# The V and B projections as a fourth Strassen-Winograd pair in a float32 hybrid-layer kernel

## The chip, the cores and the metric

The kernel runs on one core of a Trainium2 chip. A core has five engines with a queue each: TensorE (PE), VectorE (DVE), ScalarE (ACT), GpSimd (POOL) and SyncE (SP, which here only issues transfers). Each works off its own queue strictly in order and waits on semaphores. The time is the device time of one execution in microseconds.

## What is computed

One layer of a hybrid decoder for a prompt of 1024 tokens and eight samples of one new token each, all in float32. D_MODEL is 1024, there are 8 heads of 64.

```python
def _mixer_layer(x, c, conv_prev, attend, w_ada, b_ada, g_pre, w_in, conv_w, g_conv, b_sb, g_attn, w_out, g_post):
    shift, scale, gate = jnp.split(jax.nn.silu(c) @ w_ada + b_ada, 3, axis=-1)
    h = _rmsnorm(x, g_pre) * (1 + scale[:, None]) + shift[:, None]
    p = h @ w_in                                       # 1024 x 4096
    hc, bc, cc, gc, q, k, v, ga = jnp.split(p, _split_points(), axis=-1)
    u = cc * hc
    u_pad = jnp.concatenate([conv_prev.astype(u.dtype), u], axis=1)
    conv_y = sum(conv_w[i] * u_pad[:, i:i + L] for i in range(CONV_WIDTH))
    ya = _rmsnorm(bc * conv_y, g_conv) * jax.nn.silu(gc)
    o = attend(q, k, v, b_sb).reshape(Bsz, L, ATT_DIM)
    yb = _rmsnorm(o, g_attn) * jax.nn.silu(ga)
    m = jnp.concatenate([ya, yb], axis=-1) @ w_out
    y = x + gate[:, None] * _rmsnorm(m, g_post)
```

`attend` is stick-breaking attention: scores z, then exp(log_sigmoid(z) + the sum of log_sigmoid(-z) over the later keys), then times v. For the samples K and V are 4096 past rows, gathered page by page from a cache of 134 MB in use. Besides y, the kernel returns k, v and the last rows of u.

## The kernel before

**Layout.** `hT` holds h with channels on partitions: 8 blocks (K tiles) of 128 channels by 1032 columns (1024 tokens and 8 samples). Work goes through four groups g of 128 output channels (two heads). Each group needs eight projections of h, each with a 1024 x 128 slab of w_in, held in four slots of `wsl`: Q, K, V, GC, GA, HC, CC, BC (here: B).

**Seven-product pairs.** In before, six of the eight are made in three pairs: Q with K, GC with GA, HC with CC. A pair is a 2 x 2 block product by the Strassen-Winograd scheme: instead of eight block products it makes seven. The sums of h (T1 to T4, in `xT4`) are made once by DVE; the sums of the weights (S1, S2, S4 and a difference in place, 128 x 512 each) are made for each pair by POOL in `weight_sum`, four operations. The 1032 columns of a half are cut in two, so a pair has two chunks. `product(i, j)` is product j of chunk i: four matmul calls of 258 columns, into the PSUM bank `BANK[j]`. They come in the order 1, 5, 2, 6, 3, 7, 4. ACT takes products 1, 5, 2, 6 and 4 out of PSUM (`evac_st`), DVE takes 3 and 7 and adds (`product_sum`). Product 4 of a chunk waits for DVE's sum of its 7 (semaphore `d_c22`), product 5 of the next for the sum of its 3 (`d_c12`), product 2 for ACT's copy of 1 (`st_seed`).

**V and B.** V is made in before with tokens on partitions (`values`: 64 calls of 128 columns and 8 for the sample rows), since attention wants it so. B is a plain projection (`project_b`: 3 column chunks x 8 K tiles, 344 columns each).

**The program of a group.** PE's `body` has a head (t = 0 to 7) and then slots 8 to 33, where u = t - 8 numbers 24 units of attention. In the head of group 1 to 3 PE makes the Q/K pair (`EARLY`) and V; in a slot it makes scores, P.V (`outputs`), the transposes of weights (`turn`), pieces of products (`pieces_at`); in slots 32 and 33 and behind them stands B. In the first group the head projects Q and K plainly. Samples run beside it: SP loads K and V pages into `ring`, POOL multiplies a K pair by the query (`prod`, 128 x 1024), DVE reduces it (`reduce_pair`), two pairs a slot in slots 0 to 5 and then about one; PE multiplies V pages (`value_quad`). DVE also does each unit's clamp, scan and subtraction, and, in t = 0 to 6 of a head, the six `gating` steps for the group before. `gates` makes the adaLN gate, in the first group at t = 0 and 5.

Nothing is scheduled by a program: the order on each engine is the order of these loops. Behind group 3 stands the output projection: `out_unit` n makes half a token tile from 8 blocks of `yT` with 8 blocks of w_out (`wo`). The blocks of groups 0 to 2 were written to `y_parts` in memory and are loaded again.

The code below has the functions that the diff touches.

## Time and profile before

| | us |
|---|---|
| median of 3 runs | 828.92 |
| lowest, highest | 827.64, 829.51 |
| the profiled execution | 829.45 |
| its span in the trace | 827.7 |
| PE busy | 786.0 |
| DVE busy | 537.8 |
| POOL busy | 429.5 |
| ACT busy | 352.2 |

The page of the profile gives busy times by engine, the timeline gives each instruction's start and length, with the idle time before it and what ended that in brackets. A line number names the line that issues it; L1359 is the helper that issues every matmul of PE, so operations are told apart by their operands. One matmul call of float32 shows as two instructions in the trace (16 calls as x32). On PE a row's length runs a little over into the next row's start, so durations here are taken from start to start. The granted clock is 1.00 in all stretches between 60 and 787 us.

### The profile page before, as it was taken

The page shows a single profiled execution, that of the slowest core. Times are in us where ns is not written, and L with a number is a line of the kernel's source. Part 1 is how long each engine was busy: PE and PEld are TensorE (multiplying, and loading weights), DVE is VectorE, ACT ScalarE, POOL GpSimd, SP SyncE. Part 2 cuts the span into 40 slices and gives each one's busy share as a digit, 9 for nine tenths or more (in the row PEclk, how much of TensorE's full clock was granted, in tenths as well). Part 3 has the DMA queues.
Part 4 walks back from the last instruction along what each step waited for, and adds up shares of the span by engine and source line. Part 5 has one row for each costly group of instructions (what it writes and reads, how often), then busy time and mean ns, then how long its engine had stood idle before and what let it go on. Part 6 is the DMA issues. An engine that isn't in the chain of part 4 may idle for free.

```text
span 827.7 us, 14401 instructions
## 1 busy us (share of the span) xinstructions
PE 786.0 (95%) x4397; PEld 522.3 (63%) x4397; DVE 537.8 (65%) x728; ACT 352.2 (43%) x729; POOL 429.5 (52%) x230
## 2 busy tenths in 40 slices
PE   0889989999999999999999999999999999999995
PEld 0455766766787666768866766788676665444442
DVE  3575679787585888848748877585788854232344
ACT  7311065775122667821155676112567731122122
POOL 0105896474787566666966485588665630100000
PEclk9989999999999999999999999999999999999998
DMA  8998777577789888786998776868978797554001
GB/s 317 359 340 293 224 229 223 177 239 230 239 256 305 268 257 266 242 253 211 299 282 262 244 259 222 274 212 289 302 250 255 232 332 304 166 182 163 27 27 53
DMA packets 131071, 197.85 MB, mean 239 GB/s; under 512 B 10025, under 2 KB 51030, under 8 KB 130994
## 3 DMA queue, kind: packets, MB, share of 16 engines
q1 hardware_dynamic: 99512, 181.11, 66.5%
q10 hardware_dynamic: 31482, 15.82, 6.8%
q8 instruction: 35, 0.57, 0.3%
q14 instruction: 42, 0.34, 0.1%
HBM read 185.25 MB, written 11.66 MB: 238 GB/s over the span
## 4 chain that ended last, share of the span: by engine, by line
PE 79%; issue 5%; DMA 5%; DVE 4%; POOL 3%; SPq 2%; ACT 0%; ACTq 0%; POOLq 0%; DVEq 0%
PE ps L1359 76%; DMA ring<-in_w_ada_dram 4%; PE ps L1599 3%; POOL prod L617 2%; SPq L386 1%; DVE ps L1243 1%; DMA ring<-in_cache_k_dram 1%; SPq L378 1%; DVE zd L1219 1%; DVE zc L1249 0%; POOL wsl L600 0%; DVE rows L1062 0%; DMA ring<-in_cache_v_dram 0%; DVE zc L1229 0%; POOL spd L560 0%
## 5 line engine op out<-in xcount | busy, mean ns | idle before, releaser
L617 POOL TENSOR_TENSOR prod<-ring,qb 128x1024 f32<-128x1024 f32 x128 | 308.7, 2430 | 195.2 <-DMA ring<-in_cache_k_dram 92.0
L1359 PE MATMUL ps<-hT,wsl 128*128 128x258 f32 (+1 forms) x640 | 174.7, 419 | 0.1
L1219 DVE TENSOR_REDUCE zd<-prod 128x16 f32<-128x1024 f32 x128 | 154.3, 1213 | 26.0 <-POOL prod L617 25.4
L1359 PEld LDWEIGHTS ps<-hT,wsl 128*128 128x128 f32 x640 | 119.1, 190 | 53.3 <-issue 18.6
L1359 PE MATMUL ps<-ring,apad 128*32 128x512 f32 x592 | 84.4, 650 | 9.0 <-DMA ring<-in_w_ada_dram 7.5
L1359 PE MATMUL ps<-xT,wS 128*128 128x258 f32 x352 | 92.2, 385 | 0.0
L1359 PE MATMUL ps<-xT,wsl 128*128 128x258 f32 x352 | 89.5, 386 | 0.0
L1229 DVE TENSOR_SCALAR zc<-ps,bsb 128x512 f32<-128x512 f32 (+3 forms) x96 | 54.8, 612 | 42.0 <-PE ps L1359 41.7
L657 ACT ACTIVATE rise<-ps,bsh 128x512 f32<-128x512 f32 (+3 forms) x96 | 55.5, 578 | 45.9 <-DVE zc L1229 45.8
L1359 PEld LDWEIGHTS ps<-xT,wsl 128*128 128x128 f32 x352 | 62.9, 190 | 18.7 <-issue 8.0
L657 ACT ACTIVATE av<-ps 128x512 f32<-128x512 f32 (+3 forms) x96 | 46.8, 488 | 63.4 <-PE ps L1599 62.9
L1243 DVE TENSOR_TENSOR_SCAN ps<-rise,ps 128x512 f32<-128x512 f32 (+3 forms) x64 | 65.5, 1023 | 11.8 <-ACT ps L657 11.8
L1359 PEld LDWEIGHTS ps<-xT,wS 128*128 128x128 f32 x352 | 62.2, 190 | 15.4 <-issue 8.7
L1359 PEld LDWEIGHTS ps<-wsl,hT 128*128 128x128 f32 (+1 forms) x576 | 63.3, 181 | 7.6 <-issue 6.4
L1359 PE MATMUL ps<-wsl,hT 128*128 128x128 f32 (+1 forms) x576 | 66.7, 276 | 0.6 <-ACT bcb L657 0.6
L1249 DVE TENSOR_TENSOR zc<-zc,ps 128x512 f32<-128x512 f32 (+3 forms) x96 | 52.9, 551 | 2.2
L1599 PE MATMUL ps<-ident,zc 128*128 128x128 f32 x288 | 47.7, 275 | 6.6 <-DVE zc L1249 6.6
L650 POOL TENSOR_TENSOR rs<-ss,half 128x1 f32<-128x1 f32 x8 | 4.3, 544 | 90.0 <-DVE ss L1341 90.0
L657 ACT ACTIVATE sp<-zc 128x512 f32<-128x512 f32 (+3 forms) x96 | 49.7, 518 | 0.0
L657 ACT ACTIVATE ps<-sp 128x512 f32<-128x512 f32 (+3 forms) x96 | 47.5, 495 | 3.0
L1599 PEld LDWEIGHTS ps<-ident,zc 128*128 128x128 f32 x288 | 36.0, 141 | 19.4 <-DVE zc L1249 11.3
L1359 PEld LDWEIGHTS ps<-av,vN 128*64 128x64 f32 x576 | 30.5, 136 | 27.6 <-issue 25.8
(241 smaller groups left out, 1012.7 us busy)
## 6 DMA issues: line engine op xcount, KB each, us to landing
ring<-in_cache_k_dram SPq DMA_DIRECT2D x256, 256.0 KB, 3.5
ring<-in_cache_v_dram SPq DMA_DIRECT2D x256, 256.0 KB, 3.2
wsl<-in_w_in_dram ACTq DMA_DIRECT2D x30, 512.0 KB, 6.5
ring<-in_w_ada_dram SPq DMA_DIRECT2D x5, 2048.0 KB, 14.7
xT<-in_x_prompt_dram SPq DMA_DIRECT2D x2, 2048.0 KB, 10.9
out_dram<-oT SPq DMA_DIRECT2D x8, 512.0 KB, 5.0
ring<-in_x_prompt_dram SPq DMA_DIRECT2D x8, 512.0 KB, 7.2
xT<-y_parts SPq DMA_DIRECT2D x6, 512.0 KB, 9.5
```

What stands on the lines that cost most here:

```text
L378: _, numbers = nc.values_load_multi_w_load_instructions(pages[0:1, bass.ds(seq * PAGES + (PAGES - 2 - r), 2)], engines=[mybir.EngineType.S ...
L386: sp_e.dma_start(dst[:, j, :], src).then_inc(full, 16)
L617: pool.tensor_tensor(prod[:, p % 2].rearrange("p (j c) -> p j c", j=2), kring[:, p % 4], qb[:, p // 16].unsqueeze(1).to_broadcast([P, 2, H ...
L650: pool.tensor_tensor(rs[:, 20 + t % 2:21 + t % 2], ss[:, 20 + t % 2:21 + t % 2], half[:, 0:1], ALU.pow).then_inc(m_rstd, 1)
L657: nc.scalar.activation(out, in_, func, **kw).then_inc(done, 1)
L1219: v.tensor_reduce(zd[:, t // 16, :, r:r + 2], prod[:, t % 2].rearrange("p (j h d) -> p h j d", j=2, h=NH), AX_X, ALU.add)\
L1229: v.tensor_scalar(zc[:, u % 3, lo:QC], ps[:, Z + u % 3, 0:QC - lo], bsb[:, bass.ds(2 * g + h, 1)], CLAMP, ALU.add, ALU.min).then_inc(zc_re ...
L1243: v.tensor_tensor_scan(back(sums), back(rise[:, par_, lo + 1:QC + 1]), back(sums), start, ALU.add, ALU.add).then_inc(scan_done, 1)
L1249: v.tensor_tensor(zc[:, u % 3, lo:QC], zc[:, u % 3, lo:QC], sums, ALU.subtract)\
L1359: return nc.tensor.matmul(out, l, r, start=start, stop=stop, skip_group_check=True)
L1599: last = nc.tensor.transpose(ps[:, Z + u % 3, P * j:P * (j + 1)], zc[:, u % 3, lo + P * j:lo + P * (j + 1)], ident[:, :])
```

## The change

V and B become a fourth pair. A group now has four pairs and eight chunks: Q/K, V/B, GC/GA, HC/CC. `values`, `project_b` and their copies `evac_v` and `evac_b` go. V now comes out with channels on partitions (`vT`, over `av`), and is transposed by PE in eight 128 x 128 blocks and one of 8 rows (`value_rows` at t = 7 and 9, into bank Z+2, copied by ACT in `value_rows_copy`). The weight sums of V/B are made by DVE (`value_weight_sum`), the other three pairs' by POOL.

Products 1, 5, 2, 6 of the next group's first chunk (`AHEAD`) take B's place in slots 32, 33 and behind; the other 24 and product 1 of chunk 4 stand in the head. In the last group the first two blocks of `out_unit(2)` stand at slot 32. In the first group the second `gate_sums` stands behind product 1 of chunk 2. Two parts of `y_parts` and two slabs of w_out are loaded in slots 30 and 26 of the last group, the others in another order; three parts go to `kring` and not to `yT`. The attention weights of the samples are packed so that the matmuls of V pages have 8, 16, 24 or 32 columns of weights instead of 32, which leaves one clearing copy per eight samples' sequences out.

```diff
-EARLY = ((), (1, 5), (2, 6), (3, 7, 11), (4, 15), (12, 16), (13, 17))
+AHEAD = (1, 5, 2, 6)
+EARLY = ((3, 7, 11), (4, 15, 12, 16), (13, 17, 21), (14, 25, 22, 26), (23, 27, 31), (24, 35), (32, 36), (33, 37))
+EARLY_FIRST = {6: (21, 25, 22, 26, 23, 27, 31), 7: (24, 35, 32, 36, 33, 37)}
+TAKEN = {1: (4, 11, 15, 12, 16), 3: (14, 21, 25, 22, 26), 5: (24, 31, 35), 6: (32, 36)}
+TAKEN_FIRST = {6: (21, 25, 22, 26), 7: (24, 31, 35, 32, 36)}
+SUMMED = {1: 0, 3: 1, 5: 2, 8: 3}
+SUMMED_FIRST = {7: 2, 8: 3}
...
+            def value_weight_sum(g, step):
+                n = PAIRS * g
...
+                if step == 0:
+                    v.wait_ge(w_full[3], 16 * (2 * g + 1))
+                    v.wait_ge(q_out, 16)
+                    if n:
+                        v.wait_ge(st_full[5], 2 * n)
+                    v.tensor_tensor(S1, a21, a22, ALU.add).then_inc(vb_sum, 1)
+                if step == 1:
+                    v.wait_ge(w_full[2], 16 * (2 * g + 1))
+                    v.wait_ge(vb_sum, 4 * g + 1)
+                    if n:
+                        v.wait_ge(st_full[6], 2 * n)
+                    v.tensor_tensor(S2, S1, a11, ALU.subtract).then_inc(vb_sum, 1)
+                if step == 2:
+                    if n:
+                        v.wait_ge(st_full[3], 2 * n)
+                    v.wait_ge(vb_sum, 4 * g + 2)
+                    v.tensor_tensor(S4, a12, S2, ALU.subtract).then_inc(vb_sum, 1)
+                if step == 3:
+                    v.tensor_tensor(a21, a11, a21, ALU.subtract).then_inc(vb_sum, 1)
...
-                    if not first and t in (4, 6):
-                        product_sum(g, first, t // 6, 3)
-                        product_sum(g, first, t // 6, 7)
+                    chunk = (SUMMED_FIRST if first else SUMMED).get(t)
                     if u > 0 and u % 6 == 0:
...
+                        chunk = 3 + u // 6
+                    if chunk is not None:
+                        product_sum(g, first, chunk, 3)
+                        product_sum(g, first, chunk, 7)
+                    if t in (2, 3):
+                        value_weight_sum(g, 2 * (t - 2))
+                        value_weight_sum(g, 2 * (t - 2) + 1)
...
+                if not last:
+                    weight_sum(g + 1, 0, 0)
+                    weight_sum(g + 1, 0, 1)
                 silu_mul(g, 1)
                 decode_scores(g, 1, first)
                 if not last:
-                    weight_sum(g + 1, 0, 0)
+                    weight_sum(g + 1, 0, 2)
                 decode_softplus(g, 1)
                 if not last:
-                    weight_sum(g + 1, 0, 1)
+                    weight_sum(g + 1, 0, 3)
...
+                    elif last_:
+                        if u == NU:
+                            out_unit(2, (0, 1), True)
                     else:
-                        project_b(u - NU, range(0, 4))
+                        product(g + 1, 0, AHEAD[2 * (u - NU)])
...
+                    if last and t == SLOTS - 2:
+                        sp_e.wait_ge(part_out, 32 * (GROUPS - 1))
+                        sp_e.wait_ge(st_full[5], ALL)
+                        load_part(0, 0)
+                        load_part(0, 1)
+                    if last and t == 26:
+                        sp_e.wait_ge(st_full[2], CHUNKS * GROUPS - 4)
+                        load_wo(WO_ORDER[0])
+                        sp_e.wait_ge(st_full[4], CHUNKS * GROUPS - 4)
+                        load_wo(WO_ORDER[1])
...
+            sp_e.wait_ge(part_out, 32 * (GROUPS - 1))
+            sp_e.wait_ge(prod_ready, 32 * GROUPS - 3)
+            load_part(1, 0)
+            sp_e.wait_ge(prod_ready, 32 * GROUPS - 2)
+            load_part(1, 1)
             sp_e.wait_ge(z_full, NU * GROUPS)
-            load_wo(WO_ORDER[0])
-            load_wo(WO_ORDER[1])
...
             load_wo(WO_ORDER[2])
             load_wo(WO_ORDER[3])
```

**Place 1: DVE in the head of group 1**, t = 1 to 3 of its loop. `zd<-prod` is a reduction for a K pair, `qT` and `kT<-ps,stage` are the sums of products 3 and 7 of a chunk, `last` to `hcb<-hcb,bcb` step 2. Before:

```order
L1219 TENSOR_REDUCE zd<-prod 128x8x2 [waits prod_ready] x2
L1180 SCALAR_TENSOR_TENSOR last<-naught,ub 128x2
L1183 COPY tail<-last 128x2 [waits last_ready]
L1184 COPY samp<-ub 128x8
L1185 COPY samp<-gcb 128x8
L1186 COPY samp<-gab 128x8
L1188 COPY samp<-bcb 128x8 [waits pj_free]
L1189 TENSOR_TENSOR hcb<-hcb,bcb 128x1024
L1219 TENSOR_REDUCE zd<-prod 128x8x2 [waits prod_ready,bconv_ready]
L1219 TENSOR_REDUCE zd<-prod 128x8x2 [waits prod_ready]
L1095 SCALAR_TENSOR_TENSOR qT<-ps,stage 128x258 [waits e_u2,st_full3]
L1102 TENSOR_TENSOR kT<-ps,stage 128x258 [waits e_p5,st_full7]
```

And after, where `wS` and `wsl` are the weight sums of V/B:

```order
L1135 TENSOR_TENSOR wS<-wsl 128x512 [waits st_full5,q_out,w_full3]
L1141 TENSOR_TENSOR wS<-wS,wsl 128x512 [waits st_full6,vb_sum,w_full2]
L1291 TENSOR_REDUCE zd<-prod 128x8x2 [waits prod_ready] x2
L1251 SCALAR_TENSOR_TENSOR last<-naught,ub 128x2
L1254 COPY tail<-last 128x2 [waits last_ready]
L1255 COPY samp<-ub 128x8
L1256 COPY samp<-gcb 128x8
L1257 COPY samp<-gab 128x8
L1259 COPY samp<-bcb 128x8 [waits e_c21]
L1260 TENSOR_TENSOR hcb<-hcb,bcb 128x1024
L1163 SCALAR_TENSOR_TENSOR qT<-ps,stage 128x250 [waits e_u2,st_full3,bconv_ready]
L1170 TENSOR_TENSOR kT<-ps,stage 128x258 [waits e_p5,st_full7]
```

The sum of chunk 1's product 7 (the last row) stands behind two weight sums that wait for PE (`st_full5`, `st_full6`) and behind gating step 2. On PE, at the same place, from product 6 of chunk 1 through products 3 and 7 and product 1 of chunk 2 to product 4 of chunk 1, which waits for that sum (`d_c22`):

```order
L1431 MATMUL ps<-xT,wS 128x258 x4
L1431 MATMUL ps<-hT,wS 128x258 [waits e_p5]
L1431 MATMUL ps<-hT,wS 128x258 x3
L1431 MATMUL ps<-xT,wsl 128x258 [waits e_u2]
L1431 MATMUL ps<-xT,wsl 128x258 x3
L1431 MATMUL ps<-hT,wsl 128x258 [waits e_c11,w_full2]
L1431 MATMUL ps<-hT,wsl 128x258 x3
L1431 MATMUL ps<-xT,wsl 128x258 [waits d_c22]
L1431 MATMUL ps<-xT,wsl 128x258 x3
```

**Place 2: DVE in the first group's head**, t = 0 to 7. `rows`, `ub` and `gab` are the gate's steps. Before, 10 reductions and then the gate:

```order
L1219 TENSOR_REDUCE zd<-prod 128x8x2 [waits prod_ready] x10
L1060 TENSOR_TENSOR rows<-ps,ub 8x512 [waits gate_ps]
L1062 TENSOR_TENSOR rows<-rows,wS 8x512 [waits gate_step]
L1065 TENSOR_TENSOR ub<-ps,ub 128x512 [waits gate_ps,gate_step]
L1067 TENSOR_TENSOR wS<-wS,ub 128x512 [waits gate_step]
L1069 MEMSET ssa 128x1024
L1219 TENSOR_REDUCE zd<-prod 128x8x2 [waits prod_ready,ssa_zero]
L1219 TENSOR_REDUCE zd<-prod 128x8x2 [waits prod_ready] x2
```

After, with four weight sums between the reductions, and the sums of chunk 2 (`av`, `bcb`) behind the gate:

```order
L1146 TENSOR_TENSOR wS<-wsl,wS 128x512 [waits vb_sum]
L1148 TENSOR_TENSOR wsl<-wsl 128x512
L1291 TENSOR_REDUCE zd<-prod 128x8x2 [waits prod_ready] x6
L1101 TENSOR_TENSOR rows<-ps,ub 8x512 [waits gate_ps]
L1103 TENSOR_TENSOR rows<-rows,gab 8x512 [waits gate_step]
L1106 TENSOR_TENSOR ub<-ps,ub 128x512 [waits gate_ps,gate_step]
L1108 TENSOR_TENSOR gab<-gab,ub 128x512 [waits gate_step]
L1110 MEMSET ssa 128x1024
L1291 TENSOR_REDUCE zd<-prod 128x8x2 [waits prod_ready,gate_step]
L1291 TENSOR_REDUCE zd<-prod 128x8x2 [waits prod_ready]
L1166 TENSOR_TENSOR av<-ps,stage 128x258 [waits e_u2,st_full3]
L1170 TENSOR_TENSOR bcb<-ps,stage 128x258 [waits e_p5,st_full7]
```

What moved: V had no sum on DVE; now product 4 of chunk 2 on PE waits for the last row.

**Place 3: PE at slots 32 and 33 of the last group.** `hT,wsl 128x344` is B, `ring,apad` V pages, `av,vN` P.V, `spd` the samples' cumulation. Before:

```order
L1359 MATMUL ps<-av,vN 64x128 x8
L1359 MATMUL ps<-ring,apad 32x512 x4
L1359 MATMUL ps<-hT,wsl 128x344 x4
L1599 MATMUL ps<-ident,zc 128x128 x4
L1359 MATMUL ps<-xT,wsl 128x258 x4
L1359 MATMUL ps<-hT,wsl 128x344 x4
L1359 MATMUL ps<-ring,apad 32x512 x4
L1359 MATMUL ps<-hT,wsl 128x344 x8
L1359 MATMUL ps<-av,vN 64x128 x8
L1359 MATMUL ps<-hT,wsl 128x344 x8
L1359 MATMUL ps<-spd,ntri 128x256
L1359 MATMUL ps<-spd,nones 128x256
```

After, `wsl,xT` to `kT,ring` are two blocks of `out_unit(2)`, whose operands SP loads:

```order
L1431 MATMUL ps<-ring,apad 16x512 x4
L1431 MATMUL ps<-wsl,xT 128x512
L1431 MATMUL ps<-wsl,ring 128x512
L1431 MATMUL ps<-qT,xT 128x512
L1431 MATMUL ps<-kT,ring 128x512
L1592 MATMUL ps<-ident,zc 128x128 x4
L1431 MATMUL ps<-xT,wsl 128x258 x4
L1431 MATMUL ps<-ring,apad 16x512 x4
L1431 MATMUL ps<-av,vN 64x128 x8
L1431 MATMUL ps<-spd,ntri 128x256
L1431 MATMUL ps<-spd,nones 128x256
L1431 MATMUL ps<-wsl,xT 128x512
```

B is gone from here, and two blocks of the output projection stand ahead of the turn, of product 4 and of the cumulation.

## Rows read from the trace of the kernel before

**Rows 1.** The page, part 1: busy us, share of the span, instructions per engine.
```profile
PE 786.0 (95%) x4397; PEld 522.3 (63%) x4397; DVE 537.8 (65%) x728; ACT 352.2 (43%) x729; POOL 429.5 (52%) x230
```

**Rows 2.** Who waited for whom, PE: us in total, times, longest us.
```profile
PE ps L1599 <- DVE zc L1249: 6.6, 8, 1.5
```

**Rows 3.** Timeline, PE, end of group 0 and group 1: start us, us, operation, count.
```profile
210.37 1.09 PE L1359 MATMUL ps<-av,vN 128*64 128x128 f32 x16
...
217.35 7.38 PE L1359 MATMUL ps<-wsl,hT 128*128 128x128 f32 x64 [0.20 <-ACT bcb L657]
224.66 1.13 PE L1359 MATMUL ps<-ring,apad 128*32 128x512 f32 x8
225.72 2.01 PE L1359 MATMUL ps<-hT,wsl 128*128 128x258 f32 x8
227.56 1.90 PE L1359 MATMUL ps<-xT,wS 128*128 128x258 f32 x8
229.30 1.90 PE L1359 MATMUL ps<-hT,wsl 128*128 128x258 f32 x8
...
259.93 1.91 PE L1359 MATMUL ps<-wsl,hT 128*8 128x128 f32 x16
261.77 0.66 PE L1631 MATMUL ps<-ident,kT 128*128 128x128 f32 x4
```

**Rows 4.** Timeline, DVE, head of group 1.
```profile
221.75 2.54 DVE L1177 SCALAR_TENSOR_TENSOR gab<-oT,par,gab 128x1024 f32<-128x1024 f32 x1
...
227.68 1.16 DVE L1180 TENSOR_TENSOR_SCAN last<-naught,ub 128x2 f32<-128x2 f32 x1
228.88 2.28 DVE L1183 COPY tail<-last 128x2 f32<-128x2 f32 x1
...
232.61 2.35 DVE L1219 TENSOR_REDUCE zd<-prod 128x16 f32<-128x1024 f32 x2
234.87 0.42 DVE L1095 SCALAR_TENSOR_TENSOR qT<-ps,stage 128x258 f32<-128x258 f32 x1
```

**Rows 5.** Timeline, DVE and POOL, head of group 0.
```profile
96.52 0.68 DVE L1060 TENSOR_TENSOR rows<-ps,ub 8x512 f32<-8x512 f32 x1 [0.47 <-PE ps L1359]
...
102.52 2.34 DVE L1219 TENSOR_REDUCE zd<-prod 128x16 f32<-128x1024 f32 x2
...
76.25 23.17 POOL L617 TENSOR_TENSOR prod<-ring,qb 128x1024 f32<-128x1024 f32 x10 [3.27 <-DVE zd L1219]
```

**Rows 6.** Timeline, PE, first group: V, gate sums, slots 9 and 11.
```profile
87.67 7.41 PE L1359 MATMUL ps<-wsl,hT 128*128 128x128 f32 x64
...
95.45 2.08 PE L1359 MATMUL ps<-ssa,e 128*8 128x512 f32 x4
...
111.74 0.33 PE L1599 MATMUL ps<-ident,zc 128*128 128x128 f32 x1 [0.85 <-DVE zc L1249]
...
117.98 0.44 PE L1599 MATMUL ps<-ident,zc 128*128 128x128 f32 x2 [1.27 <-DVE zc L1249]
```

**Rows 7.** Timeline, ACT, group 2, slots 7 and 9.
```profile
415.49 0.60 ACT L657 ACTIVATE vN<-ps 128x512 f32<-128x512 f32 x1 [10.54 <-PE ps L1359]
...
424.92 0.26 ACT L657 ACTIVATE av<-ps 128x128 f32<-128x128 f32 x1
```

**Rows 8.** SP, PE and POOL timelines and DMA issues (median us to landing), last group.
```profile
665.66 0.43 SPq L392 DMA_DIRECT2D qT<-in_w_out_dram  x1
...
668.76 2.58 PE L1359 MATMUL ps<-hT,wsl 128*128 128x344 f32 x8
...
677.76 1.46 POOL L560 TENSOR_TENSOR spd<-spd,om 128x256 f32<-128x256 f32 x1 [7.26 <-ACT om L657]
...
xT<-y_parts SPq DMA_DIRECT2D x6, 512.0 KB, 9.5
...
wsl<-in_w_out_dram SPq DMA_DIRECT2D x3, 512.0 KB, 7.8
...
qT<-in_w_out_dram SPq DMA_DIRECT2D x1, 512.0 KB, 4.6
```

493 lines of the change are left out of this document (239 added, 254 removed).

## The prediction

> **What bounds the kernel now.** First the busy times: PE works 786.0 us, 95% of the span, DVE 537.8 and POOL 429.5 [rows 1]. Then PE's waits: the largest entry that another engine causes is 6.6 us in eight waits, all for the subtraction that DVE makes for a unit's turn [rows 2]. The reader is to see that PE hardly waits: a matmul taken out shortens the kernel by nearly its time, and a wait put in front of PE lengthens it by its time. So the question is first how much PE work goes, and then which new waits of PE the new order on DVE, ACT and SP makes. For the second, the timelines of the engines around the edited places are laid over the new orders.
>
> The sum is made against the profiled execution, 829.45 us. The median of the three runs is 828.92, so the last step takes off 0.53.
>
> **PE's work.** A row runs by 0.17 or so into the next (2.01 at 225.72 against 1.84 to the next start [rows 3]). B is 24 calls, 48 instructions; 8 of them are 2.58 [rows 8] less 0.17, so B is 6 x 2.41 = 14.5 us a group. V is 64 instructions twice and 16 once: 217.35 to 224.66 is 7.31, 259.93 to 261.77 is 1.84 [rows 3], in all 16.5. Together 31.0 go. Two chunks of seven products come: a product takes from 227.56 to 229.30, 1.74 [rows 3], 14 are 24.4. Nine transposes of V come; four are 0.66 long [rows 3] less 0.17, so 0.12 each and 1.1 in all. A group saves 31.0 - 24.4 - 1.1 = 5.5, the four groups **22.0 us**. This term has one answer. The narrower weights of the page matmuls change nothing that I count: their cost lies in the 512 columns streamed, 1.06 for eight from 224.66 to 225.72 [rows 3].
>
> **DVE in the heads of groups 1 to 3** (place 1). DVE now makes V/B's second weight sum only when PE has finished product 6 of chunk 1, and sum 7 of chunk 1 stands behind it, behind two reductions and behind gating step 2. PE has three products left by then, 3 and 7 of chunk 1 and 1 of chunk 2, 3 x 1.74 = 5.2 us, and then product 4 waits for that sum. DVE needs: the weight sum, 512 columns; a sum of 258 columns takes 0.42 [rows 4], so I estimate 0.65; two reductions 2.35 [rows 4]; gating step 2 from 227.68 to 232.61, 4.93 [rows 4]; two sums at 0.42, 0.84. That is 8.8. PE waits 8.8 - 5.2 = 3.6 us, in three groups **10.7 us**. Queued behind the waiting DVE instruction is all of this, and PE alone waits for it. Before, the same sum had slack, since V's 7.31 us stood in PE's queue there. The unsure piece is the 4.93: a scan of two elements takes 1.16 in it and a copy of two elements 2.28 [rows 4]. Such small ones are long while POOL multiplies, and end as its instruction ends. Were POOL idle, neither need be longer than the 0.42 of a 258-column sum; step 2 is then 4.93 - 3.44 + 0.84 = 2.3, DVE needs 6.2 and PE waits 1.0. Bounds for the three groups: 3.0 to 10.7. I take the upper end, because POOL multiplies K pairs throughout that head as before and the rows are from the same place.
>
> **The first group's head** (place 2). There V stood in PE's queue from 87.67 [rows 6]. Now, from there: product 1 of chunk 2 (1.74), one more call of 258 columns (a quarter product, 0.44), the gate sums (2.08 at 95.45, less the 0.17: 1.9 [rows 6]), products 5, 2, 6, 3, 7 (8.7), product 1 of chunk 3 (1.74): 102.2. Then product 4 of chunk 2 waits for DVE's two sums. These stand behind gate step 2, which took from 96.52 to 102.52, and two reductions, 2.34 [rows 5]: 104.9, with the sums 105.7. PE waits 3.5. But DVE also has four weight sums of 512 columns between its reductions now. POOL's ten products there run without a gap, 23.17 us, 2.32 each [rows 5], and a reduction leaves DVE about 1.1 us between two. A step with two SBUF operands, started beside such a product, was long: gating step 1 took 2.54 in group 1 [rows 4]. If the four weight sums take turns with POOL's products, each puts the chain of products and reductions back by about half a product, 4 x 1.16 = 4.6, of which the 0.47 that DVE idled before the gate [rows 5] is to spare: 4.1, and PE waits 3.5 + 4.1 = 7.6. In return PE's waits of 0.85 and 1.27 in slots 9 and 11 [rows 6], 2.1 together, go: they are DVE's backlog behind the gate, which by then is worked off while PE waits. Net **5.5 us**, bounds 1.4 (no turns) and 5.5. I take 5.5, since the 2.54, the 1.16 and the 2.28 all show turns.
>
> The Trainium skill, "SBUF — State Buffer", section on the two separate sides, says that VectorE and GpSimd share a port pair under an exclusive lock held for a whole instruction, and that a VectorE operation with two SBUF inputs needs it while a reduction does not. The 2.54, 1.16 and 2.28 [rows 4] agree, and so do reductions that stay at 1.17 each. By that rule the wait in the first group is 7.6; without it it is 3.5, and the sum of all terms 4.1 us lower.
>
> **Slot 10.** ACT now copies V's four transposed tiles in one operation there; the like copy took 0.60 at 415.49 [rows 7]. It stands behind the copy of the weights, 0.26 at 424.92 [rows 7], and PE's next scores wait for the bank that it empties. PE's queue has nothing to put between, so I charge the copy whole: 4 x 0.60 = **2.4 us**. The lower bound is 0, if ACT has taken it before the weights come.
>
> **The end of the last group** (place 3). B was what PE did while SP's loads for the output projection landed. Now two blocks of it stand at 668.76 [rows 8], where B's first eight instructions were. Two parts and two w_out slabs come early; the other two parts and slabs 1 and 5 are issued where the first slab was, from 665.66. The first of such a row landed after 4.6, later ones after 7.8 [rows 8]. The fourth, issued 0.9 later, is there at 674.4. PE has done 1.7 us of blocks at 670.5 and waits 3.9. Then come the blocks left, 1.7, the turn, 0.5, product 4, 1.74, a page group, 1.06, and P.V, about 1.0 [rows 3, 8]: 680.4, and PE's cumulation needs POOL's 1.46 us product of 677.76, which followed ACT's logarithms [rows 8]. ACT takes product 4 out before them; that copy can now start only at 678.3, and with 0.4 for it, 1.6 for the four functions and 1.46 for POOL the operand is there at 681.8. PE waits 1.4 more. **5.3 us**, bounds 0.7 (the fourth lands after 4.6, no second wait) and 7.0 (it lands after 9.5, as loads of parts did [rows 8]). I take the row of the nearest position in the queue.
>
> Costed at nothing: POOL loses four of its weight sums a group; SP's earlier loads in slots 26 and 30 cover the same bytes; the clearing copies that go were not on PE's path. If DVE's longer queue in the heads reached slot 8, that would cost; see the slow rival.
>
> **The sum.** 829.45 - 22.0 + 10.7 + 5.5 + 2.4 + 5.3 = 831.35, and 0.53 off is **830.8 us**.
>
> **Rivals.** (1) *The waits are light.* DVE's steps run at their undisturbed times, where the columns allow, the loads land early, and slot 10 costs nothing: 828.9 - 22.0 + 3.0 + 1.4 + 0 + 0.7 is 812.0; with DVE's term in the heads at full size, or with the three others so, it is 819 to 821, with one more 824. For it speaks that POOL has less to do in the head than before, against it the three long rows. (2) *No new waits at all*, the pure saving: 828.9 - 22.0 = 806.9; for it only that PE's waits were tiny so far. (3) *Between*, 824 to 827: the DVE term is at two thirds. (4) *Slower: DVE does not recover by slot 8.* In a head of groups 1 to 3 DVE gets two weight sums in a row in t = 2 and two in t = 3, beside 16 reductions of 1.17 and the gating. If each waits out a whole product of POOL, 2.32, instead of half, PE's wait at chunk 1 grows by 2.3 us, and the first clamp of slot 8 comes, by my estimate, 1 us late: 3.3 in three groups is 9.9, so 840.7. It decides from the point where a weight sum takes over 1.2 us on average. For it: the copy of two elements that took 2.28 [rows 4]. Against it: POOL too waits for DVE's reductions and then leaves gaps. (5) The change not doing what it says is excluded as far as products go: the calls are in the order.
>
> **How the numbers follow.** A measurement of this kernel tells 0.2%, 1.7 us, from no change, so no change is 827.3 to 830.6. The forecast's own range is 827.3 to 835, chance 0.40, of it 0.18 within no change and 0.22 above. Rival 1 has 0.20 and rival 3 0.14, both faster; rival 2 and the lowest part of rival 1 have 0.07, faster. Rival 4, 836 to 841, has 0.15. The 0.04 left go to no change. Faster 0.41, no change 0.22, slower 0.37. The range from 819.0 to 838.0 holds all but rival 2, the lowest part of rival 1 and the upper half of rival 4.
>
> **What would show it.** PE's busy time down by about 22, products at 1.74. In groups 1 to 3 a row of PE with about 3.6 us idle before product 4 of chunk 1, ended by DVE's sum. In the first group 3.5 (no turns) or 7.6 (turns) before product 4 of chunk 2, with DVE's weight sums 0.65 or well over 1 us. No wait of 0.85 and 1.27 in slots 9 and 11. In slot 10 about 0.6, ended by ACT's copy of V. In the last group about 3.9 us before the third or fourth block, ended by a load, and about 1.4 before the cumulation. The forecast is wrong first if gating step 2 is much shorter than 4.93 in the new order, since most of what eats the saving hangs on it and on the 7.6.

## The result and the profile after

| | before | after |
|---|---|---|
| median, us | 829.21 | 845.62 |
| lowest, highest (4 runs each) | 827.64, 830.87 | 845.47, 846.80 |
| span of the profiled execution | 827.7 | 843.9 |
| PE busy | 786.0 | 776.7 |
| span less PE busy | 41.7 | 67.2 |
| mean granted clock of TensorE | 0.992 | 0.976 |

The ratio is 1.0193, with a 95% interval of 1.0174 to 1.0212: the change makes the kernel slower by 1.9%. The page of the kernel after, part 1, busy us per engine, answers to [rows 1]:

```profile
PE 776.7 (92%) x4113; PEld 515.0 (61%) x4113; DVE 563.6 (67%) x760; ACT 359.2 (43%) x749; POOL 433.2 (51%) x230
```

PE is busy 9.3 us less and idle 25.5 us more. That makes the 16.2 us of the span. The view of PE's waits (us in total, times, longest), which answers to [rows 2], names the idle time:

```profile
PE ps L1431 <- DVE kT L1170: 11.4, 3, 3.8
...
PE ps L1592 <- DVE zc L1321: 10.1, 8, 2.5
PE ps L1431 <- DVE bcb L1170: 7.7, 1, 7.7
...
PE ps L1431 <- DMA ring<-y_parts: 3.3, 1, 3.3
...
PE ps L1431 <- issue: 1.1, 1, 1.1
```

The three waits of 3.8 us for the sum of product 7 of chunk 1 (kT), the one of 7.7 us in the first group (bcb), and the 3.3 and 1.1 us at the end of the last group were not there before. The waits for the turn's operand went from 6.6 to 10.1 in all.

PE's busy time holds the surprise. 22.0 us less work were forecast, 9.3 less are seen. The timeline of PE in the first group and in group 2 (start us, us, operation, count, in brackets the idle time before it) shows where the rest is:

```profile
109.26 3.81 PE L1431 MATMUL ps<-xT,wsl 128*128 128x258 f32 x8 [7.71 <-DVE bcb L1170]
112.86 2.28 PE L1431 MATMUL ps<-xT,wS 128*128 128x258 f32 x8
114.98 1.90 PE L1431 MATMUL ps<-hT,wsl 128*128 128x258 f32 x8
```

```profile
408.42 3.81 PE L1431 MATMUL ps<-xT,wsl 128*128 128x258 f32 x8 [3.81 <-DVE kT L1170]
412.02 2.88 PE L1431 MATMUL ps<-xT,wS 128*128 128x258 f32 x8
414.74 1.90 PE L1431 MATMUL ps<-hT,wsl 128*128 128x258 f32 x8
```

A product at full speed takes 1.74 from start to start, as in [rows 3]. Behind the wait of 7.71 the first one takes 3.60 (109.26 to 112.86) and the second 2.12. Behind the 3.81 of group 2 they take 3.60 and 2.72. The windows of group 2 (us; busy us of PE, PEld, DVE, ACT, POOL; then the granted clock, the DMA share and GB/s) show the clock:

```profile
402.00:404.00 2.00, 2.00 (x10) 1.74 (x10) 1.97 (x3) 0.00 (x0) 2.00 (x2) 1.00 0.90 313
404.00:406.00 2.00, 0.61 (x3) 0.19 (x1) 2.00 (x1) 0.00 (x0) 2.00 (x1) 1.00 0.57 152
406.00:408.00 2.00, 0.00 (x0) 0.00 (x0) 1.97 (x8) 0.00 (x0) 0.14 (x1) 0.79 0.51 187
408.00:410.00 2.00, 1.58 (x4) 1.30 (x5) 2.00 (x5) 0.00 (x0) 0.00 (x0) 0.50 0.81 242
...
412.00:414.00 2.00, 2.00 (x6) 1.61 (x5) 0.78 (x1) 0.76 (x2) 2.00 (x2) 0.50 0.71 253
414.00:416.00 2.00, 2.00 (x10) 1.75 (x10) 0.91 (x2) 0.39 (x1) 2.00 (x2) 1.00 0.86 242
```

PE stops at 404.6. The clock is 1.00 up to 406, falls while PE waits (0.79 in 406 to 408) and is 0.50, the lower of the two levels (1.2 GHz), until 414, 5.6 us into the work. Then it is 1.00 again. Over all places where it is low behind a wait, start to start against 1.74 a product (0.86 a block of the output projection): 2.2 us in the first group, 1.5, 2.8 and 2.9 in groups 1 to 3, 1.8 in the last group's end. Another 1.7 is lost at 724 to 728, just behind the samples' sums of one column, behind no wait. Together 12.9, and 22.0 - 12.9 is the 9.1 that PE's busy time fell.

That last 1.7 costs the kernel little. Behind the same place the kernel before waits for a V page, and the kernel after, which comes there later, does not (first before, then after):

```profile
714.41 1.13 PE L1359 MATMUL ps<-ring,apad 128*32 128x512 f32 x8 [1.53 <-DMA ring<-in_cache_v_dram]
```

```profile
731.02 1.06 PE L1431 MATMUL ps<-ring,apad 128*8 128x512 f32 x8
```

The Trainium skill, "TensorE: Matmul & The Clock Gate", part 1, says that the array runs at half clock by default and that activity releases it, so that idle gaps bring the lower clock back and work behind them starts slow. The rows agree: 0.50 behind the wait of 3.81 in group 2.

DVE's timeline in the head of group 1 is what [rows 4] were before:

```profile
241.80 0.69 DVE L1141 TENSOR_TENSOR wS<-wS,wsl 128x512 f32<-128x512 f32 x1 [2.12 <-PE ps L1431]
...
244.66 1.47 DVE L1251 TENSOR_TENSOR_SCAN last<-naught,ub 128x2 f32<-128x2 f32 x1
246.17 2.27 DVE L1254 COPY tail<-last 128x2 f32<-128x2 f32 x1
...
250.23 0.42 DVE L1170 TENSOR_TENSOR kT<-ps,stage 128x258 f32<-128x258 f32 x1
...
280.63 0.61 DVE L1301 TENSOR_SCALAR zc<-ps,bsb 128x128 f32<-128x128 f32 x2 [2.63 <-PE ps L1431]
```

Gating step 2 (from the scan at 244.66 to the sums) lies between the reductions and the sum of product 7 at 250.23, just as it was forecast: 5.2 us long (249.90, where the sums begin, less 244.66) where 4.93 was charged, with the same two-element copy of 2.27. The last row is the first clamp of slot 8, which waits 2.63 us for PE: DVE was not late there.

In the first group's head ([rows 5]) the four weight sums of V/B, 128 x 512 each, lie between the reductions:

```profile
77.24 1.99 DVE L1135 TENSOR_TENSOR wS<-wsl 128x512 f32<-128x512 f32 x1
79.33 2.66 DVE L1141 TENSOR_TENSOR wS<-wS,wsl 128x512 f32<-128x512 f32 x1
...
84.17 2.00 DVE L1146 TENSOR_TENSOR wS<-wsl,wS 128x512 f32<-128x512 f32 x1
86.09 2.84 DVE L1148 TENSOR_TENSOR wsl<-wsl 128x512 f32<-128x512 f32 x1
```

They take 1.99 to 2.84, and the second one of group 1, at 241.80 with POOL idle, takes 0.69. They did take turns with POOL's products, as the prediction chose. At the end of the last group, where [rows 8] had B:

```profile
696.52 1.29 PE L1431 MATMUL ps<-wsl,xT 128*128 128x512 f32 x2 [3.33 <-DMA ring<-y_parts]
...
707.23 0.67 PE L1431 MATMUL ps<-spd,ntri 128*128 128x256 f32 x2 [1.13 <-issue]
```

The wait of 3.33 is ended by the load of a part, and it stands ahead of the first block and not ahead of the third or fourth, where it was forecast. The code says why: a part's load for either half of the channels counts up the same semaphore (`part_in[k]`), and block 0 waits until both have come, so the load issued in slot 30 alone does not let it start. The other was issued at 690.16, and the block starts 6.4 us later. The fourth block has its operands in time.

### The profile page after: what moved, and what is told of

The parts are those of the page before. It is cut to its first block, busy times and chain, and to the rows that moved or that the text cites. A ratio compares the mean times of both kernels' runs of the same rounds, so it can differ in the third digit from the quotient of the medians.

```text
span 843.9 us, 13952 instructions
## 1 busy us (share of the span) xinstructions
PE 776.7 (92%) x4113; PEld 515.0 (61%) x4113; DVE 563.6 (67%) x760; ACT 359.2 (43%) x749; POOL 433.2 (51%) x230
## 4 chain that ended last, share of the span: by engine, by line
PE 70%; DVE 10%; issue 7%; DMA 4%; SPq 4%; POOL 3%; ACT 1%; POOLq 0%; DVEq 0%; ACTq 0%
PE ps L1431 66%; PE ps L1592 3%; DVE zd L1291 2%; POOL prod L659 2%; DMA xT<-in_x_prompt_dram 2%; SPq L413 1%; SPq L405 1%; DMA ring<-in_w_in_dram 1%; DVE ps L1315 1%; DMA ring<-y_parts 1%; DMA ring<-in_cache_k_dram 1%; DVE xT L1066 1%; POOL wsl L644 1%; DVE wS L1141 1%; DVE last L1251 0%
## 5 line engine op out<-in xcount | busy, mean ns | idle before, releaser
L1431 PE MATMUL ps<-hT,wsl 128*128 128x258 f32 (+1 forms) x576 | 145.7, 397 | 0.3 <-DVE zb L1189 0.3
L1431 PE MATMUL ps<-xT,wsl 128*128 128x258 f32 x480 | 127.7, 403 | 19.2 <-DVE kT L1170 11.4
L1431 PEld LDWEIGHTS ps<-hT,wsl 128*128 128x128 f32 x576 | 107.8, 191 | 33.1 <-issue 12.0
L1431 PE MATMUL ps<-xT,wS 128*128 128x258 f32 x480 | 125.2, 391 | 0.0
L1431 PEld LDWEIGHTS ps<-xT,wsl 128*128 128x128 f32 x480 | 91.2, 199 | 47.2 <-DVE kT L1170 12.7
L1431 PEld LDWEIGHTS ps<-xT,wS 128*128 128x128 f32 x480 | 88.5, 195 | 20.9 <-issue 10.1
L1431 PE MATMUL ps<-ring,apad 128*32 128x512 f32 (+3 forms) x592 | 81.8, 632 | 7.2 <-DMA ring<-in_w_ada_dram 7.1
L702 ACT ACTIVATE av<-ps 128x512 f32<-128x512 f32 (+4 forms) x104 | 49.9, 480 | 84.0 <-PE ps L1592 70.6
L1431 PE MATMUL ps<-hT,wS 128*128 128x258 f32 x240 | 62.3, 391 | 0.0
L1592 PE MATMUL ps<-ident,zc 128*128 128x128 f32 x288 | 47.8, 275 | 10.1 <-DVE zc L1321 10.1
L1431 PEld LDWEIGHTS ps<-hT,wS 128*128 128x128 f32 x240 | 42.5, 190 | 19.0 <-issue 14.6
## 6 DMA issues: line engine op xcount, KB each, us to landing
ring<-in_w_ada_dram SPq DMA_DIRECT2D x5, 2048.0 KB, 14.3
xT<-in_x_prompt_dram SPq DMA_DIRECT2D x2, 2048.0 KB, 11.2
```

The source lines that it names most:

```text
L702: nc.scalar.activation(out, in_, func, **kw).then_inc(done, 1)
L1431: return nc.tensor.matmul(out, l, r, start=start, stop=stop, skip_group_check=True)
L1592: last = nc.tensor.transpose(ps[:, Z + u % 3, P * j:P * (j + 1)], zc[:, u % 3, lo + P * j:lo + P * (j + 1)], ident[:, :])
```

## The experiments

Each kernel was timed beside the kernel before on the same chip. The differences below are between medians. They come from three chips, on which the kernel before took 829.57 (the runs up to all three places mended), 830.74 (the transfers moved, and the narrow weights) and 829.00 (the rest). Where versions from different chips are compared, the difference of their ratios, taken on 829 us, is given too. Fills and moves are told from the changed kernel (845.6).

### The waits filled with work

```diff
-                        product(g, code // 10, code % 10)
+                        product(g, code // 10, code % 10, again={21: 0 if first else 2, 31: 4 if first else 0}.get(code, 0))
...
-                for k in ks:
+                for k in list(ks) * (1 + again):
```

> The changed kernel, but PE makes product 1 of V/B's second chunk three times over in groups 1 to 3, and product 1 of the third chunk five times over in the first group: 2 x 1.74 us in place of each wait of 3.8 us, 4 x 1.74 in place of the 7.7. The repeats overwrite the same bank, so nothing else changes. Theory A (a wait of PE is paid a second time, because TensorE's granted clock is at half speed for some us behind it): the waits become work of the same length and the slow matmuls behind four of the five waits, 2.2 + 1.5 + 2.8 + 2.9 = 9.4 us by the profile of the changed kernel, go. About 836. Theory B (PE's surplus of 12.7 us has another cause, and a matmul more is only a matmul more): 845 to 846, since work stands where a wait stood.

Measured 839.96, ratio to before 1.0128 [1.0104, 1.0151], 5.7 less than the changed kernel though PE has ten products, 17.4 us, more to make. Its timeline of PE in group 1 (the repeats, then product 4):

```profile
246.95 5.38 PE L1431 MATMUL ps<-hT,wsl 128*128 128x258 f32 x24
252.68 2.01 PE L1431 MATMUL ps<-xT,wsl 128*128 128x258 f32 x8 [0.35 <-DVE kT L1170]
```

Product 4 at 252.68 now takes 1.85 from start to start behind a wait of 0.35. Work in place of a wait made the kernel faster, which theory B excludes. The gain is less than the 9.4 of theory A: PE's busy time rose by 13.1 (to 789.8), not by 17.4 - 9.4 = 8.0. Of the missing 5.1, 1.7 is slow clock behind a wait of 2.45 us in slot 13 of the first group, after which the clock did not fall in the changed kernel (2.54 there), and some 3.3 is slow clock in the prologue of this execution, ahead of the edit (32 small matmuls there took 5.88 in place of 3.92, 16 of another kind 3.30 in place of 1.92).

### DVE's sums ahead of gating step 2

```diff
-SUMMED = {1: 0, 3: 1, 5: 2, 8: 3}
+SUMMED = {1: 0, 5: 2, 8: 3}
...
+                    if not first and t == 2:
+                        product_sum(g, first, 1, 3)
+                        product_sum(g, first, 1, 7)
                     if not first and t in GATING_AT:
```

> The changed kernel with one edit: in groups 1 to 3 DVE makes the two sums of V/B's... rather of chunk 1 (Q/K) ahead of gating step 2, not behind it. DVE is through with its reductions at 244.66 in the profile of the changed kernel, PE has product 7 done at 245.0 and wants the sum at 246.7. Theory A: the three waits of 3.8 us (11.4) go, and with them the slow clock behind them (7.2): 845.6 - 18.6 = 827. Theory B: only the waits go: 834. Theory C (DVE is the bound in the head and the wait comes back at the next sum or in slot 13): 840 or more.

Measured 841.84, ratio 1.0151 [1.0129, 1.0173]: only 3.8 less. The waits of PE:

```profile
PE ps L1595 <- DVE zc L1324: 13.9, 8, 4.1
PE ps L1434 <- DVE bcb L1170: 10.7, 4, 7.7
```

The entry for kT is gone, as it should. But the waits for the turn's operand rose from 10.1 to 13.9, most of it in slot 13 (4.1, 3.1 and 2.7 in groups 1 to 3, against 1.6, 1.9 and 1.9), and a wait of 1.0 in each of these groups came for the sum of chunk 2, behind gating step 3 (bcb, 10.7 in all with the 7.7). The clock now falls to 0.50 behind slot 13. So the gain was given back some 46 us later (the wait of 3.8 began at 246.9 in group 1, the one of 4.1 at 293.3), wait and slow clock together: theory C, in another place than the next sum.

### DVE's sums ahead of the second gate step, first group

```diff
-SUMMED_FIRST = {7: 2, 8: 3}
+SUMMED_FIRST = {8: 3}
...
+                    if first and t == 5:
+                        product_sum(g, first, 2, 3)
+                        product_sum(g, first, 2, 7)
                     if first and t in (0, 5):
                         gates(t // 5)
```

> The changed kernel with one edit: in the first group DVE makes the two sums of chunk 2 ahead of the second gate step, not behind it. Theory A: the wait of 7.7 us shrinks to 0.5 (DVE can start the second sum at about 101.4) and the 2.2 us of slow clock go: 845.6 - 9.4 = 836. Theory B: only the wait goes: 838.4. The gate step then comes 1.5 us later; if PE's transposes of K wait for it, or DVE's backlog grows by slot 13, some of it comes back (up to 2).

Measured 837.06, ratio 1.0090 [1.0065, 1.0115]: 8.6 less, between A's 9.4 and B's 7.2. In the profile the wait of 7.7 has no row left, and the clock is 1.00 between 60 and 240 us. Nothing came back in this group.

### All three places mended

```diff
-                    elif last_:
-                        if u == NU:
-                            out_unit(2, (0, 1), True)
-                    else:
+                    elif not last_:
                         product(g + 1, 0, AHEAD[2 * (u - NU)])
...
-                if not last_:
+                if last_:
+                    out_unit(2, (0, 1), True)
+                else:
                     product(g + 1, 0, AHEAD[3])
                 cumulate(1)
```

with the two edits above.

> Both edits of DVE's order, and the two blocks of the output projection moved from slot 32 of the last group to just ahead of the last cumulation, where their loads have landed. Theory A: all of 11.4 + 7.2, 7.2 + 2.2 and about 4.4 + 1.8 go: 845.6 - 34 = 811 to 813. Theory B: only waits go: 845.6 - 23 = 822.6. Theory C (new waits behind the removed ones): above 825.

Measured 828.05, ratio 0.9977 [0.9949, 1.0004], not to be told from before, and its ten runs spread from 821.4 to 830.7, for a reason that the one trace kept does not show. Against theory A 15 us are missing. PE waits 14.6 us for the turn's operand, up to 3.8 in slot 13 of each group. The chain there, in group 1, read backwards. PE, DVE and POOL in their timelines:

```profile
289.54 0.55 PE L1598 MATMUL ps<-ident,zc 128*128 128x128 f32 x3 [3.77 <-DVE zc L1327]
```

```profile
286.81 1.22 DVE L1297 TENSOR_REDUCE zd<-prod 128x16 f32<-128x1024 f32 x1 [4.29 <-POOL prod L659]
```

```profile
277.82 1.27 POOL L644 TENSOR_TENSOR wsl<-wsl 128x512 f32<-128x512 f32 x1
284.44 2.34 POOL L659 TENSOR_TENSOR prod<-ring,qb 128x1024 f32<-128x1024 f32 x1 [5.35 <-issue]
```

PE waits for DVE's subtraction, DVE's reduction at 286.81 waited 4.29 for POOL's product, and POOL stood from 279.1 to 284.4 with nothing that the profile names. Its operand is a pair of K pages. SP's queue and ACT's, and the issues of 272 to 276 with their KB and median us to landing:

```profile
274.58 0.43 SPq L479 DMA_DIRECT2D out_dram<-vN  x1
276.24 4.51 SPq L413 DMA_DIRECT2D ring<-in_cache_k_dram  x4
```

```profile
273.40 0.38 ACTq L767 DMA_DIRECT2D wsl<-in_w_in_dram  x1
```

```profile
wsl<-in_w_in_dram ACTq DMA_DIRECT2D x1, 512.0 KB, 8.2
out_dram<-vN SPq DMA_DIRECT2D x1, 512.0 KB, 8.4
```

The pages are issued from 276.24. Just ahead of them go the store of V's rows (the vN row) and a load of weights, 512 KB each, which take over 8 us here (6.1 and 4.7 in the kernel before). In the kernel before, the store stood at 267.57 and the load at 261.88, and pages issued at 269.21 let POOL start at 273.70, 4.5 us after their issue against 8.2 here. The store stood as close ahead of the pages then (1.6 us) as it does now (1.7). What moved is the load: 7.3 us ahead of the pages before, 2.8 now, since its slab is free only when chunk 3 is done. So two transfers and not one stand right ahead of the pages of slots 11 and 12.

### The two transfers moved, each alone and together

```diff
-                    if t == 10:
+                    if t == 14:
                         sp_e.wait_ge(pj_free, PJ * g + 2)
```

> The version with all three edits (a_all3), and SP's store of V's rows (512 KB) moved from slot 10 to slot 14, behind the K page loads of slots 11 to 13. In a_all3 PE waits 14.6 us in eight waits for the turns, 2.1, 3.8, 3.5 and 3.2 us of it in slot 13 of each group; there DVE's reduction waits 4.3 us for POOL's product, and that for a K page pair, which lands 8.2 us after its issue, behind the store of V at 274.6 and a load of weights at 273.4. Theory D1 (the store is what delays the pages): the slot 13 waits fall to 1 us or less and the slow clock behind them goes: 828 - 9 - 7 = 812. Theory D2 (the load of weights does): same as a_all3. Theory E (DVE or POOL have too much work in slots 8 to 13): same as a_all3.

```diff
-                    if i == 3:
+                    if i == 4:
                         load_w(g, CC_, 3)
```

> The version with all three edits (a_all3), and ACT's load of the CC weights (512 KB) issued before its copy of product 4 of chunk 4 (about slot 14) and not of chunk 3 (slot 10). Theory D2 (that load delays the K pages of slots 11 and 12): slot 13 waits fall, 812 to 818. Theory D1 (the store does) and theory E (DVE's or POOL's work): same as a_all3.

```diff
-SUMMED = {1: 0, 5: 2, 8: 3}
+SUMMED = {1: 0, 8: 3}
...
-                    if not first and t == 2:
-                        product_sum(g, first, 1, 3)
-                        product_sum(g, first, 1, 7)
+                    if not first and t in (2, 4):
+                        product_sum(g, first, t // 2, 3)
+                        product_sum(g, first, t // 2, 7)
```

> Both of these moves, and DVE's sums of chunk 2 ahead of gating step 3 (PE waits 1.0 us there in each of groups 1 to 3 in a_all3). Theory D1 or D2: at least the better of the two, less 3 us: 808 to 812. Theory E: 825.

| | median | ratio to before | waits for the turn's operand |
|---|---|---|---|
| all three mended | 828.05 | 0.9977 [0.9949, 1.0004] | 14.6 |
| and the store later | 818.99 | 0.9870 [0.9823, 0.9918] | 8.2 |
| and the load later | 814.01 | 0.9783 [0.9748, 0.9818] | 8.4 |
| and both, and the sums of chunk 2 | 812.85 | 0.9782 [0.9744, 0.9820] | 5.7 |

The waits are those of the profiled execution. For the version with the load moved that was the slowest of five (819.32), with 3.3 of its 8.4 in one wait in group 2. By the ratios, on 829 us, moving the store gains 8.9 and moving the load 16.1. Moving either transfer brings most of the waits down, and neither D1 nor D2 holds alone, since each expected nothing of the other move: the pages were late because two transfers of 512 KB stood ahead of them. With both moved, and the sums of chunk 2, the time is not to be told from the load moved alone (0.9782 and 0.9783). Theory E falls, since no engine has less work in these three kernels. POOL in the best one, at the same place (the weight sum, then the product that was at 284.44, 4.6 us behind its pages' issue at 274.40), and its waits of PE:

```profile
276.78 1.27 POOL L644 TENSOR_TENSOR wsl<-wsl 128x512 f32<-128x512 f32 x1
279.04 2.38 POOL L659 TENSOR_TENSOR prod<-ring,qb 128x1024 f32<-128x1024 f32 x1 [0.99 <-issue]
```

```profile
PE ps L1598 <- DVE zc L1327: 5.7, 8, 1.1
...
PE ps L1437 <- DMA rise<-in_w_out_dram: 1.3, 1, 1.3
```

This version beats both kernels: 17.9 us or 2.2% less than the kernel before on the same chip. From PE's first scores of one group to those of the next it takes 152.3 and 153.3 us (265.48, 417.76, 571.03) where the kernel before took 157.2 and 157.9, so a group gained 4.8 of the 5.5 us that its products save.

### A wait put back, short and long

```diff
+                    for i in range(more):
+                        v.tensor_tensor(S2, S1, a11, ALU.subtract).then_inc(vb_sum, 1)
+                        v.wait_ge(vb_sum, at + 2 + i)
                     v.tensor_tensor(S2, S1, a11, ALU.subtract).then_inc(vb_sum, 1)
```

with more = 3 and 8 in groups 1 to 3, in the best version; the counts that DVE and PE wait for are raised to match. The run with 8 is told first. Its expectation says "the same" of the edit with 3, whose expectation stands behind it.

> The same with nine in place of one: the sum comes 5.6 us later, PE waits some 4.4 us three times. Theory A: 13.2 of waits and 2.9 of slow clock behind each (as behind the waits of 3.8 in the changed kernel): 812.9 + 13.2 + 8.6 = 834.7. Theory B (a wait is paid once): 826. If DVE's delay reaches slots 8 to 13, both more.

Measured 829.07, ratio 1.0015 [0.9997, 1.0034]: 16.2 more than the best version. PE waits 4.39 three times, 13.2:

```profile
239.84 3.60 PE L1442 MATMUL ps<-xT,wsl 128*128 128x258 f32 x8 [4.39 <-DVE kT L1175]
243.24 2.04 PE L1442 MATMUL ps<-xT,wS 128*128 128x258 f32 x8
245.11 1.90 PE L1442 MATMUL ps<-hT,wsl 128*128 128x258 f32 x8
```

The two products behind the wait take 3.40 and 1.87, 1.8 us more than two at full speed. So each of these waits cost 4.4 and about 1.8 more where I expected 2.9, and 13.2 + 5.4 is 18.6 against 16.2 between the medians (16.0 between the spans; two rows of the prologue took 3.5 longer in the best version's profiled execution, 3.64 against 1.92 and 5.52 against 3.71). The clock falls behind every one of them. The two versions ran on different chips. By their ratios (1.0015 and 0.9782, with intervals of 0.0018 and 0.0038 to either side) the difference is 19.3 us, give or take 3.5 by my estimate from these intervals. That holds the 18.6 and leaves out theory B's 13.2. Theory A holds in kind, with a second price that varies from 1.5 to 2.9 us in these traces.

> The best version so far (b_best, 812.9 us), in which PE waits nowhere over 1.4 us between 60 and 800 us, and DVE makes V/B's second weight sum four times over in groups 1 to 3 (the same result, each about 0.7 with its semaphore). The sum of product 7 of chunk 1 then comes 2.1 us later, some 1.0 after PE wants it. Theory A' (a short wait is paid once, only a long one is paid twice): 812.9 + 3.0 = 816. Theory A'' (any wait lowers the clock): 816 + 3 x 2 = 822.

Measured 820.29, ratio 0.9890 [0.9865, 0.9914]: 7.4 more than the best version, 9.0 by the ratios, where A' expected 3.0 and A'' 9.

```profile
PE ps L1603 <- DVE zc L1332: 9.6, 13, 1.9
...
PE ps L1442 <- DVE kT L1175: 2.3, 3, 0.8
```

The waits put in are 0.75 each, 2.3 in all, and the clock is 1.00 behind them: A'' falls, though its sum came nearer to the time. For PE also waits 3.9 us more for the turn's operand, in 13 places and not 8, with one of 1.9 at 296.4, behind which the clock falls (1.7 us). PE's first scores of group 1 come 0.9 us later than in the best version (266.39 against 265.48), and the K pages of 283.76 are asked for 1.7 us later, at 285.42. That is seen. Why it costs more than the shift of 4.4 us in the run above (5.6 for the turn's operand) stays open.

### The output blocks back at slot 32

The best version without the move of out_unit(2).

> b_best with the two blocks of the output projection back at slot 32 of the last group, as in the changed kernel. Theory A: a wait of 3.3 to 4.5 us for the parts and 1.1 for the cumulation come back, with 1.8 us of slow clock: 812.9 + 6.5 = 819. Theory B (only the wait): 817.5. If the loads are in time here, 813.

Measured 817.07, ratio 0.9845 [0.9813, 0.9876], 4.2 more than the best version, 5.2 by the ratios. The waits of PE:

```profile
PE ps L1437 <- DMA ring<-y_parts: 4.5, 1, 4.5
...
PE ps L1437 <- issue: 1.1, 1, 1.1
```

The wait for the part and the one for the cumulation are back, 5.6 together, and the clock is 0.60 and 0.55 in the two windows of 2 us behind the first (668 to 672). With 1.7 lost to the clock that makes 7.3. The time shows less, but the two intervals, together 4 us wide to either side, do not tell theory A's 6.5 more from theory B's 4.6. The wait for the part stands ahead of the first block again, as in the changed kernel. Only the one for the cumulation is the wait that the prediction described.

### V/B's weight sums on POOL

In the changed kernel, value_weight_sum is moved word for word from DVE to POOL, at the start of its slots 2 and 3.

> The changed kernel with the four weight sums of V/B on POOL (at the start of its slots 2 and 3 after the products of slot 1 and 2) and not on DVE. In the changed kernel the four of the first group last 2.0 to 2.8 us each on DVE beside POOL's products, against 0.7 undisturbed. Theory P (the two engines take turns, so that it hardly matters which makes them): the wait of 7.7 in the first group stays above 5, and 842 to 846. Theory Q (DVE's queue is the bound, and POOL has time): the first group's wait falls to 3.5 and the three of 3.8 to 3.1 or less: 845.6 - 4.2 - 2 and less slow clock, 835 to 839.

Measured 839.13, ratio 1.0114 [1.0087, 1.0141], 6.5 less than the changed kernel:

```profile
PE ps L1592 <- DVE zc L1321: 14.0, 8, 3.4
...
PE ps L1431 <- DVE bcb L1173: 8.6, 1, 8.6
```

Neither theory holds whole. The three waits of 3.8 for kT are gone altogether, since DVE no longer waits for PE's product 6 ahead of its reductions and gating step 2. And step 2 itself is short now, for POOL is idle while it runs (it waits for product 6 from 241.7 to 243.2). DVE's scan and copy of two elements in group 1, which took 1.47 and 2.27 in the changed kernel:

```profile
241.67 0.15 DVE L1251 TENSOR_TENSOR_SCAN last<-naught,ub 128x2 f32<-128x2 f32 x1
241.85 0.17 DVE L1254 COPY tail<-last 128x2 f32<-128x2 f32 x1
```

Step 2 takes 1.8 us here and 5.2 there. That is the choice that the prediction had to make between 2.3 and 4.93, shown from both sides: in these traces the two instructions were long only beside POOL's products. The wait in the first group rose to 8.6, since POOL's products came later by its four sums of 1.26 each: for this wait it hardly matters which of the two engines makes them, as P has it. And slot 13 took part of the gain, as with the sums moved.

### The narrow weights

```diff
-                rows_ = NH * (BATCH - seq % BATCH)
+                rows_ = NH * BATCH
```

> a_all3 with the matmuls of V pages at 32 columns of weights for every sample, as before the change, and not at 8 to 32 (the surplus columns hold other samples' weights, so the samples' rows of the output are not computed rightly). In a_all3 TensorE's granted clock falls to 0.5 at 707 us with no wait ahead of it, in the stretch of 16 sums of one column and of matmuls with 8 columns of weights; in the kernel before it does not. Theory W (the narrow weights bring it about): the clock stays at 1.0 there, about 1.7 us less. Theory X (the pattern of waits or of loads before it): it falls as in a_all3.

Measured 825.42 in a single execution, within the spread of the version that it was made from (821.42 to 830.71), so the time says nothing. The clock stays at 1.00 in the stretch of one-column sums and behind it, as in the kernel before. With the narrow weights it falls there, by 1.7 us, in ten of the twelve profiles: not in the version with the load moved, nor in the one with the sums on POOL. One execution against ten of twelve leans to W and does not show it. The cause stays open. Its price is small either way. In the four profiles in which the clock stays at 1.00 there (the kernel before, this one and the two exceptions), PE then waits 1.53 to 1.65 us for a V page, and in the ten others at most 0.85.

## Why the prediction was wrong

The prediction was 830.8, with a range from 819.0 to 838.0, and the time is 845.6. By its own steps:

| step | forecast, us | in the trace |
|---|---|---|
| PE's work | -22.0 | -22 (busy -9.3 with 12.9 of slow clock taken out) |
| waits in the heads of groups 1 to 3 | 3 x 3.6 = 10.7 | 3 x 3.8 = 11.4 |
| wait in the first group | 7.6 | 7.7 |
| waits in slots 9 to 14, all groups | -2.1 | +3.5 |
| slot 10 | 2.4 | 0, no row |
| end of the last group | 3.9 + 1.4 | 3.3 + 1.1 |
| slow clock behind waits | not in the sum | 11.2, and 1.7 behind none |
| PE's other waits | not in the sum | -1.5 in all, with 1.53 less for the V page |

**PE's work.** Right: a product takes 1.74, and the best version shows the saving in each group (4.8 of 5.5 with what is left of waits).

**The new waits.** Those in the heads, in the first group and before the cumulation were named with their place and releaser, and all sizes came within 0.7 us. The wait at the output blocks was right in size by luck: 3.9 was worked out for the fourth block and its load issued last, and 3.33 was waited ahead of the first block, for a part, which the prediction took to be there in time. The two choices between bounds, gating step 2 at its full 4.93 (5.2 measured) and turns between DVE and POOL, were both right. Idle time of PE rose by 25.5 where the terms gave 23.9.

**The step that failed** is the first one: "a matmul taken out shortens the kernel by nearly its time, and a wait put in front of PE lengthens it by its time". The second half is false here. A wait of 3.3 to 7.7 us was paid a second time by 1.5 to 2.9 us lost to matmuls at half clock, 11.2 us in all behind five waits. Without it the kernel would have taken 845.6 - 11.2 = 834.4, inside the range. The filled waits and the long wait put back show it from both sides. The kernel before gave a hint that I passed over: its page has the clock below full speed in the prologue, where PE waits, and I took the 1.00 between 60 and 787 us as a property of the stretch and not of a PE that never stopped for long there. Between 60 and 787 us the largest wait in it that DVE caused is 1.5 us [rows 2]. The prediction calls that entry the largest that another engine causes. In the whole view it is not: DVE causes a wait of 10.5 us in the prologue. No sum rests on it.

**The second step that failed** is the credit of 2.1 us for waits that would be worked off ([rows 6]). While PE waits, DVE does catch up, and the waits of 0.85 and 1.27 are gone. But one of 2.54 came in slot 13 of the first group, and the others grew there. The waits of slots 13 and 14 hang on K pages, and these on transfers, one of which the change moved. "SP's earlier loads in slots 26 and 30 cover the same bytes" looked at the loads in the last group, and not at ACT's load of CC, which now joins the store of V ahead of the pages of slots 11 and 12. I named them nowhere. In the changed kernel the two stand at 285.47 and 286.25 in group 1, the pages are issued from 287.87, and POOL's product starts 6.4 us later, at 294.33, against 4.5 before. How much of the growth is theirs was measured only in the mended versions. The waits of these slots account for 5.6 us of the error, the slow clock for 12.9, slot 10 for -2.4, the sizes of the four named waits for -0.1, and other waits of PE, which fell, for -1.5. The V page's 1.53 is the largest of those, and takes back most of the 1.7 lost behind no wait. That is 14.5, and the span grew by 14.3 more than the terms add up to (16.2 against 1.9).

**Slot 10** was counted too high: ACT's copy of V's transposed tiles was not what PE's next scores waited for.

**The rivals.** Rival 4 came nearest with 840.7, 4.9 us short, by a mechanism that is not there: DVE had 2.6 us to spare at slot 8 of group 1. The rivals with light waits had the gain in view that only the mended version has: with the new waits gone the change is worth 2.2%, and rival 1's 812.0 stands beside the best version's 812.9. That is no credit to the rival, since the waits did not go by themselves.

## What to carry to other kernels

In a kernel whose PE is never idle for long, price a new wait of three microseconds or more at its length and some 1.5 to 2.9 us on top, and look at the granted clock in windows behind every wait before believing a busy time. When a block of PE work is taken out of a stretch, list what it covered on every queue, transfers too: a load of 512 KB that had been harmless joined a store of the same size ahead of small pages, and the delay went through three engines. And when a wait is mended and half the gain is missing, look for it in the next stage before doubting the first reading.
